# A first projection streamed into the norm before it, and masks built later, in a two-layer encoder trunk

## The reference

```
y = rms_norm(h, norm_w[0, 0])
xb, zb = split(y @ rg_w_in)                # 1024 -> 2 x 2048
xb = dwconv(xb, conv_w) + conv_b           # four taps
for d in (forward, backward):
    r, i = sigmoid(xb_blocks @ gate_w[d] + gate_b[d])       # 8 blocks of 256
    a = exp(-8 * softplus(-lam[d]) * r)
    h_d = linear_recurrence(a, sqrt(1 - a^2) * i * xb)
out = ((h_0 + h_1) * silu(zb)) @ rg_w_out
```

## Time and profile before

| | |
|---|---|
| median of 3 runs | 2765.61 us (2759.55 to 2768.03) |
| the profiled execution | 2772.26 us |
| its span in the profile | 2770.5 us |
| setup | ends at 30.0 us |
| first norm | 30.0 to 61.7 us |
| recurrent stage | 61.7 to 832.3 us |
| second norm | 832.3 to 902.1 us |
| DeltaNet projection, chunks, last norm | 902.1 us to the end |

### The profile page before, as it was taken

How to read it: one execution, slowest core, us unless ns; L and a number is a source line. 1 busy time by engine, 2 the same in 40 slices (tenths; PEclk the granted TensorE clock), 3 DMA queues, 4 the chain that set the end, 5 groups by cost and what they waited for, 6 DMA issues and landing times. The chain is left out here.

```text
span 2770.5 us, 51969 instructions
## 1 busy us (share of the span) xinstructions
PE 2569.3 (93%) x18313; PEld 2485.3 (90%) x18313; DVE 1810.4 (65%) x2713; ACT 1257.3 (45%) x2179; POOL 1215.6 (44%) x1111
## 2 busy tenths in 40 slices
PE   3999999988996999999999699999999999999994
PEld 3999999988994889999999699999999999998994
DVE  5277777777006788888888666767767777776103
ACT  4366666673013534445443345554545545465102
POOL 4333333436211255554445454545545555573320
PEclk7999999999998999999999789999999999999997
DMA  4122212123104355544454542424244241423113
GB/s 156 43 63 62 61 61 61 61 85 108 46 22 158 83 152 164 162 141 124 143 159 136 175 117 50 120 50 120 64 101 113 54 114 50 119 71 110 46 38 122
DMA packets 243118, 269.26 MB, mean 97 GB/s; under 512 B 86747, under 2 KB 210220, under 8 KB 241276
## 3 DMA queue, kind: packets, MB, share of 16 engines
q1 hardware_dynamic: 242940, 266.96, 33.5%
HBM read 182.59 MB, written 84.33 MB: 96 GB/s over the span
## 5 line engine op out<-in xcount | busy, mean ns | idle before, releaser
L649 PE MATMUL ps<-dn_yhi,dn_whi 128*128 128x348 f32 x1128 | 385.2, 341 | 8.0 <-ACT p_vrow L1548 5.3
L2281 ACT ACTIVATE zz<-ps 104x416 fp32r<-104x416 f32 x560 | 283.6, 516 | 228.6 <-PE ps L2117 226.8
L650 PE MATMUL ps<-dn_ylo,dn_whi 128*128 128x348 f32 x1128 | 363.0, 322 | 0.0
L651 PE MATMUL ps<-dn_yhi,dn_wlo 128*128 128x348 f32 x1128 | 362.9, 322 | 0.0
L2404 DVE TENSOR_TENSOR pp<-ps,level_mask 104x416 fp32r<-104x416 f32 x480 | 275.7, 588 | 132.1 <-PE ps L2117 130.1
L649 PE MATMUL ps<-rg_yhi,rg_whi 128*128 128x346 f32 (+1 forms) x960 | 310.9, 324 | 42.0 <-PEq L82 32.9
L651 PE MATMUL ps<-rg_yhi,rg_wlo 128*128 128x346 f32 (+1 forms) x960 | 310.4, 323 | 0.0
L650 PE MATMUL ps<-rg_ylo_r,rg_whi 128*128 128x346 f32 (+1 forms) x960 | 310.4, 323 | 0.0
L2119 PE MATMUL ps<-pp,zz 104*104 104x208 f32 x1440 | 267.5, 296 | 18.5 <-ACT zz L2281 9.6
L2119 PE MATMUL ps<-zz,pp 104*104 104x208 f32 x1440 | 248.4, 283 | 0.0
L649 PEld LDWEIGHTS ps<-dn_yhi,dn_whi 128*128 128x128 f32 x1128 | 213.0, 189 | 13.0 <-issue 9.6
(11 more groups left out here) (356 smaller groups left out, 7025.0 us busy)
## 6 DMA issues: line engine op xcount, KB each, us to landing
c_nq<-nq_scratch SPq DMA_DIRECT2D x160, 169.0 KB
dn_raw<-in_dn_w_in SPq DMA_DIRECT2D x48, 512.0 KB, 4.4
qd<-rows_scratch SPq DMA_DIRECT2D x160, 104.0 KB, 3.1
rg_raw<-in_rg_w_in SPq DMA_DIRECT2D x32, 512.0 KB, 4.4
nq_scratch<-p_nq SPq DMA_DIRECT2D x48, 338.0 KB
p_ex<-rows_scratch SPq DMA_DIRECT2D x32, 422.5 KB
nq_scratch<-p_rn SPq DMA_DIRECT2D x32, 338.0 KB
n_h<-h_scratch SPq DMA_DIRECT2D x16, 520.0 KB, 7.6
```

The source lines that it names most:

```text
L649: e.matmul(o, whi, mhi[:, t0:t0 + tn], start=(first and k == 0), stop=False)
L650: e.matmul(o, whi, mlo[:, t0:t0 + tn], start=False, stop=False)
L651: ins = e.matmul(o, wlo, mhi[:, t0:t0 + tn], start=False, stop=(last and k == end))
L2281: e.activation(zz[:, b, :, :], ps[0:CH, 2 * b + 1, 0:m4], ACT.Copy).then_inc(zev.sem, 1)
```

## The change

Four things change.

The weights of X0 and X1 of turn 0 are loaded in the setup, between token rows 5 and 6, and GpSimd splits them there. In the first norm PE multiplies each tile k by both units, 18 matmuls a tile, into PSUM banks 0 to 2 and 3 to 5, as soon as `rg_ylo` of that tile is written. In the same phase SyncE loads the weights of X0 and X1 of turn 1 ahead of the stores of `h_first`; they are split at the recurrent stage's start, and PE's first unit there is X0 of turn 1.

The level masks leave the setup. GpSimd builds them with the same 57 operations behind its last weight split of the recurrent stage.

The setup holds seven token rows, and ScalarE's squares alternate between two buffers.

`row_diag` is made by VectorE, behind its copy of the same row, and no longer by ScalarE.

```diff
--- before.py
+++ after.py
@@ -167,10 +167,11 @@
             with ExitStack() as s2:
                 h = sb(s2, "h_first", [P, KT, T])
                 setup(nc, sb, ps, c, x, meta_tokens, norm_w, rg_conv_w, rg_conv_b, rg_gate_b, rg_lambda,
-                      dn_conv_w, dn_norm_w, h)
+                      dn_conv_w, dn_norm_w, h,
+                      (room, [rg_w_in[0].rearrange("(k p) m -> p k m", p=P)[:, :, j * P:(j + 1) * P] for j in (0, 1)]))
                 norms(nc, sb, ps, c, "n0", h_dram, None, None, 0, 0, yhi, ylo, h=h,
                       first=(room, [rg_w_in[0].rearrange("(k p) m -> p k m", p=P)[:, :, j * P:(j + 1) * P]
-                                    for j in (0, 1)]))
+                                    for j in (2, 3)]))
             rg_loop(nc, sb, ps, c, yhi, ylo, room, rg_w_in, rg_gate_w, o_dram, rg_w_out, y, ysum, twin,
                     o_raw)
         base = (nc.sbuf_base + 31) // 32 * 32
@@ -206,13 +207,13 @@
 
 
 def setup(nc, sb, ps, c, x, meta_tokens, norm_w, rg_conv_w, rg_conv_b, rg_gate_b, rg_lambda,
-          dn_conv_w, dn_norm_w, ht):
+          dn_conv_w, dn_norm_w, ht, first):
 
     with Phase(nc) as s:
         prow = sb(s, "prow", [P, 3, P])
-        ROWS = 4
+        ROWS = 7
         hrow = sb(s, "hrow", [CH, ROWS, D])
-        junk, ssq, diag = sb(s, "row_sq", [CH, D]), sb(s, "row_ssq", [CH, NC]), sb(s, "row_diag", [CH, 2, CH])
+        junk, ssq, diag = sb(s, "row_sq", [CH, 2, D]), sb(s, "row_ssq", [CH, NC]), sb(s, "row_diag", [CH, 2, CH])
         tmp, work = sb(s, "sp_tmp", [P, 4, 32]), sb(s, "sp_work", [P, 4, 32])
         sem = lambda n: s.semaphore(n)
         par_in, masks, par_t, par_done = sem("par_in"), sem("masks"), sem("par_t"), sem("par_done")
@@ -220,6 +221,7 @@
         ident_ready, row_t, row_free = sem("ident_ready"), sem("row_t"), sem("row_free")
         row_sq, diag_done, row_sum = sem("row_sq"), sem("row_diag"), sem("row_sum")
         act_done, dve_done = sem("sp_act"), sem("sp_dve")
+        w_in, w_hi, w_lo = [sem("w_in0"), sem("w_in1")], sem("w_hi"), sem("w_lo")
         block = s.block()
 
         @block.sync
@@ -241,6 +243,10 @@
                 if k >= ROWS:
                     e.wait_ge(row_t, k - ROWS + 1)
                     e.wait_ge(row_sq, k - ROWS + 1)
+                if k == 6:
+                    for j in range(2):
+                        e.dma_start(first[0][0][:, j, :].rearrange("p (k m) -> p k m", k=KT), first[1][j]) \
+                            .then_inc(w_in[j], 16)
                 if k == 0:
                     e.dma_start(hrow[0:META, 0, :], meta_tokens).then_inc(row_in[0], 16)
                     e.dma_start(hrow[META:CH, 0, :], x[0, 0:CH - META, :]).then_inc(row_in[0], 16)
@@ -283,22 +289,12 @@
             select(gm[:, 1, 0, :], ALU.is_gt, 0.0, 0, 1, [[-1, CH]])
             select(gm[:, 0, 1, :], ALU.is_ge, 0.0, 0, -1, [[1, CH]])
             select(gm[:, 1, 1, :], ALU.is_ge, 0.0, 0, 1, [[-1, CH]])
-            lm = c["level_mask"]
-            then(e.memset(lm[:, :, :, :], 0.0))
-            for l in range(LEVELS):
-                m = 1 << l
...
-                    select(lm[:, l, d, :], ALU.not_equal, 1.0, 0, 1, [[-1, P]])
+            raw, hi, lo = first[0]
+            for j in range(2):
+                e.wait_ge(w_in[j], 16)
+                e.tensor_copy(hi[:, j, :], raw[:, j, :]).then_inc(w_hi, 1)
+                e.wait_ge(w_hi, j + 1)
+                e.tensor_tensor(lo[:, j, :], raw[:, j, :], hi[:, j, :], ALU.subtract).then_inc(w_lo, 1)
 
         @block.tensor
         def _(e):
@@ -345,6 +341,11 @@
                 src = ps[:, 2 * (k % 2):2 * (k % 2) + 2, 0:4 * CH].rearrange("p a (b t) -> p a b t", t=CH)
                 dst = ht[:, :, k * CH:(k + 1) * CH].rearrange("p (a b) t -> p a b t", b=4)
                 e.tensor_copy(dst, src).then_inc(row_free, 1)
+                e.wait_ge(row_sq, k + 1)
+                if k >= 2:
+                    e.wait_ge(row_sum, k - 1)
+                e.tensor_scalar(diag[:, k % 2, :], c["ident"][0:CH, 0:CH], ssq[:, k:k + 1], None, ALU.mult) \
+                    .then_inc(diag_done, 1)
 
         @block.scalar
         def _(e):
@@ -370,13 +371,41 @@
             e.activation(tmp[:, 2, :], lam, ACT.Relu, scale=-1.0).then_inc(act_done, 1)
             for k in range(NC):
                 e.wait_ge(row_in[k % ROWS], 16 * (k // ROWS + 1 + (k % ROWS == 0)))
-                e.activation(junk[:, :], hrow[:, k % ROWS, :], ACT.Square, accum_out=ssq[:, k:k + 1]) \
+                if k >= 2:
+                    e.wait_ge(row_sq, k - 1)
+                e.activation(junk[:, k % 2, :], hrow[:, k % ROWS, :], ACT.Square, accum_out=ssq[:, k:k + 1]) \
                     .then_inc(row_sq, 1)
-                e.wait_ge(row_sq, k + 1)
-                if k >= 2:
-                    e.wait_ge(row_sum, k - 1)
-                e.activation(diag[:, k % 2, :], c["ident"][0:CH, 0:CH], ACT.Copy, scale=ssq[:, k:k + 1]) \
-                    .then_inc(diag_done, 1)
+
+
+def level_masks(e, lm, done):
+
+
+    count = [0]
+
+    def then(ins):
+        count[0] += 1
+        ins.then_inc(done, 1)
+        e.wait_ge(done, count[0])
+
+    def select(view, op, fill, base, ch, pattern):
+        then(e.affine_select(out=view, in_=view, compare_op=op, fill=fill, base=base,
+                             pattern=pattern, channel_multiplier=ch))
+
+    then(e.memset(lm[:, :, :, :], 0.0))
+    for l in range(LEVELS):
+        m = 1 << l
+        nb = P // (2 * m)
+        v = [lm[:, l, d, :].rearrange("p (b h j) -> p b h j", h=2, j=m)[:, :, d, :] for d in (0, 1)]
+        for d in (0, 1):
+            then(e.memset(v[d], 1.0))
+
+        select(v[0], ALU.is_ge, 0.0, -m, 1, [[-2 * m, nb], [0, m]])
+        select(v[0], ALU.is_ge, 0.0, 2 * m - 1, -1, [[2 * m, nb], [0, m]])
+
+        select(v[1], ALU.is_ge, 0.0, 0, 1, [[-2 * m, nb], [0, m]])
+        select(v[1], ALU.is_ge, 0.0, m - 1, -1, [[2 * m, nb], [0, m]])
+        for d in (0, 1):
+            select(lm[:, l, d, :], ALU.not_equal, 1.0, 0, 1, [[-1, P]])
 
 
 def softplus(e, work, expo, relu, at, done):
@@ -435,7 +464,7 @@
         def _(e):
             for j in range(2) if first else ():
                 e.dma_start(first[0][0][:, j, :].rearrange("p (k m) -> p k m", k=KT), first[1][j]) \
-                    .then_inc(w_in[j], 16)
+                    .then_inc(w_next, 16)
             for k in range(KT) if yt is None else ():
                 e.dma_start(h_dram[k], ht[:, k, :]).then_inc(stored, 16)
             if ab:
@@ -447,6 +476,7 @@
                 e.dma_start(ht[:, k, :], h_dram[k]).then_inc(h_in[k], 16)
             if yt is None:
                 e.wait_ge(stored, 16 * KT)
+                e.wait_ge(w_next, 32)
             elif pre is not None:
                 for k in range(KT):
                     e.wait_ge(added, k + 1)
@@ -508,6 +538,15 @@
                                        sq[:, k % 2, t0:t0 + tn] if src is ht else ysum[:, t0:t0 + tn],
                                        start=(k == 0), stop=(k == n - 1))
                     ins.then_inc(summed, 1)
+            for k in range(KT) if first else ():
+                e.wait_ge(lo_done, k + 1)
+                for j in range(2):
+                    _, whi, wlo = first[0]
+                    for b, (t0, tn) in enumerate(EVEN):
+                        o, cols = ps[:, 3 * j + b, 0:tn], slice(k * P, (k + 1) * P)
+                        e.matmul(o, whi[:, j, cols], yhi[k][:, t0:t0 + tn], start=(k == 0), stop=False)
+                        e.matmul(o, whi[:, j, cols], ylo[k][:, t0:t0 + tn], start=False, stop=False)
+                        e.matmul(o, wlo[:, j, cols], yhi[k][:, t0:t0 + tn], start=False, stop=(k == KT - 1))
             if ab:
                 _, whi, wlo = lead[0]
                 e.wait_ge(ab_lo, 1)
@@ -570,8 +609,8 @@
                 e.wait_ge(ab_hi, 1)
                 e.tensor_tensor(ab["lo"][:, :, :], ab["raw"][:, :, :], ab["hi"][:, :, :], ALU.subtract) \
                     .then_inc(ab_lo, 1)
-            for j in range(2) if first or lead else ():
-                raw, hi, lo = (first or lead)[0]
+            for j in range(2) if lead else ():
+                raw, hi, lo = lead[0]
                 e.wait_ge(w_in[j], 16)
                 e.tensor_copy(hi[:, j, :], raw[:, j, :]).then_inc(w_hi, 1)
                 e.wait_ge(w_hi, j + 1)
@@ -676,7 +715,7 @@
 
 
     with Phase(nc) as s:
-        wt = Weights(nc, sb, s, "rg", (1, 1, 2, 2, 1, 1), 2, ahead=2, room=room, come=1)
+        wt = Weights(nc, sb, s, "rg", (1, 1, 2, 2, 1, 1), 2, ahead=2, room=room, come=2)
         (xpad, o1), (xc, o2), (zs, o15) = twin(s, "xpad", [P, 2, T + 4]), twin(s, "xc", [P, 2, T]), twin(s, "zs", [P, 2, T])
         (xhi_raw, xhi), (xlo_raw, xlo) = twin(s, "xhi", [P, 2, T]), twin(s, "xlo", [P, 2, T])
         a, u = (y[:, 4 * i:4 * i + 4, :].rearrange("p (d t) x -> p d t x", d=2) for i in (0, 1))
@@ -689,7 +728,8 @@
```

(7 more changed lines are left out.)

9 lines of the change are left out of this document (removed).

## The result

The changed kernel took 2773.0 us, the median of 20 runs (2762.1 to 2785.6), against 2765.6 for the kernel before (20 runs, 2759.6 to 2771.7). The ratio is 1.0030, with a 95% interval of 1.0022 to 1.0039: it is slower by about 0.3%, where 0.42% faster was forecast. The profiled execution took 2773.2, its span 2771.4.

What follows compares the result with a forecast made beforehand. PE was taken to bound the kernel, busy for 2569.3 of 2770.5 us. The terms -14.96 + 3.0 + 0.3 = -11.7 us took the median from 2765.61 to 2753.9, with a range of 2745 to 2764.

Steps and rivals of the forecast that it cites:

- The step that failed: Recurrent stage's start: from the first gates on, engines were taken to stand to each other as before.
- masks on the path: Recurrent stage's end: masks take 45.8 us, the stage ends 20.5 us later, 2774.4; rival's chance 0.04.
- a low clock all through the norm: First norm: PE's 144 matmuls stay at the low clock, 43.8 instead of 24.3 us, 2773.4; rival's chance 0.03.
- my sum: Whole kernel: -14.96 up to the gates, + 3.0 setup, + 0.3 masks = -11.7 us, median 2753.9.
- The setup term: Setup: two weight loads and a longer tail start the next phase 3.0 us later; bounds -0.2 and +8 us.
- a bound and a rival: Setup: VectorE's diagonals wait 2 us behind GpSimd's splits; in the +8 us bound and the 2760.2 rival, chance 0.21.
- The norm: First norm: VectorE's pair takes 2.52 us, PE starts 8.82 us in, the recurrent stage starts 35.64 us in.
- The restart: First norm: PE's start at the low clock, for nine matmuls, adds 1.30 us.
- The recurrent stage's start: There PE waits 4.05 us for GpSimd's split, then 1.30 for the clock and 22.97 of matmuls before the gates.
- This restart: Recurrent stage's start: PE's clock falls again while it waits, charged another 1.30 us.
- The masks: Recurrent stage's end: hidden by 1.4 to 2.4 us; 0.3 us charged for VectorE's two additions, bounds 0 and 3.
- the port rule: Recurrent stage's end: GpSimd and VectorE lock each other out, masks held up to 2.5 us, costing 0.1 to 1.1 more.

Runs made afterwards that it cites:

- its two forms: Changed kernel with the ten diagonals back on ScalarE, 2749.6 us; changed kernel with three one-column memsets ahead of VectorE's setup, 2757.0 us.
- the unrolled version: Changed kernel with the three turns of the chunk loop written out on every engine, so no branch goes back: 2751.7 us.

## Why the prediction was wrong

**The step that failed** is the one sentence at the end of the recurrent stage's start: "From there on all engines stand to each other as before." The sum has nothing for the chunk stage because of it. For the data flow it is nearly true. But VectorE's program was 18 instructions longer ahead of a loop that first branches back at 1874.81, and I had looked only at what instructions wait for, not at where they stand. The order of instructions of both kernels was at hand and would have given the count. None of the rivals had the mechanism; the slower ones, masks on the path (2774.4) and a low clock all through the norm (2773.4), have times that the 2773.0 comes near by chance, and neither happened. In place of the nothing, the runs showed second pauses of 5.41 and 4.53 us, and 16.0 us of time that went with them when VectorE's program was shifted by three instructions.

The two profiles give this account. 10.3 us are gained at the second norm. 3.4 are lost at three clock starts behind it, and 2.5 more at the start of the chunk stage, around which PE's clock is at its lower level for 61.4 us (from 1549.3) instead of 54.6 (from 1559.6). So the changed kernel is 4.4 ahead at the loop (1839.04 against 1843.43). 12.4 are lost at the two branches back (251.9 against 239.5). This gives 8.0 slower, and the medians say 7.4. The profiled executions themselves are only 0.9 apart, since that of the kernel before, 6.7 above its median, lost 7 us at three other steps of the chunk stage (116.7, 116.7 and 118.8 where the changed kernel has 115.1). Without the second pauses the change is worth what was forecast: 0.9943 and 0.9969 in its two forms, about 16 and 9 us, around the 11.7 of my sum. With runs of one kernel that lie 15 us apart, this bears the sum out only within some 4 us.

The Trainium skill has the rule (Runtime: NRT & Kernel Launch, on instruction fetch mechanics): the instruction memory of most engines is two blocks of 256 instructions, filled in sequence, and a taken branch to a target outside them stalls until it is fetched. The runs agree with the branch stalling (2.7 to 3.6 us on VectorE) and with a boundary that matters to one instruction; the length of a block no run here measured. Nor does a loop's length alone say whether it pays: ScalarE's of 460 instructions, fewer than two such blocks would hold, paused for 2.4 to 2.7 us, and GpSimd's of 287 did not. The Trainium skill calls the cost of crossing a boundary in that same section mostly hidden, and the unrolled version agrees, with no issue wait at `head_pair`. The second stall of a loop's head close to a boundary, which decides this case, rests on the runs alone. The prediction drew on none of this.

**The setup term**, forecast 3.0, measured 3.23, by a partly different way. Row 9 was there by 27.39 instead of 28.3, but the tail behind it took 5.1 us (27.39 to 32.52) instead of 3.4. Row 6 landed 4.7 us behind row 5, where the rows before it came 1.9 apart: SyncE's issue of the second weight load took 4.20 us and that of row 6 5.76. Rows 6 to 9 then came 1.1 to 1.5 us apart, and PE needed 1.8 for each: eight transposes took it 1.59 in rows 6 to 8, where those of row 8 took 0.93 in the kernel before. In the changed kernel with the diagonals on ScalarE they took 1.54, 1.65, 0.88 and 0.93, and the norm began at 31.98. One diagonal of VectorE also took 1.85 us instead of 0.27, beside GpSimd's split; the prediction had this only in a bound and a rival. The same loads and splits gave norm starts of 31.98 to 34.45 in other kernels, so the setup is loose by 2.5 us.

**The norm.** VectorE's pair took the 2.52 forecast, and PE began at 41.96 (forecast 41.8). The restart was sized too small: the first 18 matmuls, not 9, ran at the lower level, 5.37 us from 41.96 to 47.33, which costs 5.37 - 18 x 0.1595 = 2.50 instead of 1.30. PE ended at 67.57 (66.3), and the stage began at 69.86 (68.6).

**The recurrent stage's start.** The wait for GpSimd's split is there and as forecast: PE's first matmul 3.77 us into the stage (4.05). The first gate came at 98.67 (97.0). This restart was sized too small as well: from PE's first matmul to the gate it was 98.67 - 73.63 = 25.04, which is 2.07 above the 22.97 at the higher level, where 1.30 was charged. The gain at this point was 10.3, forecast 11.7 + 0.3.

**The masks** are hidden. GpSimd ended at 819.18 and the last addition still took 1.24 us, so the 0.3 I charged was zero, and the further price of 0.1 to 1.1 by the port rule did not appear. What the prediction cites as that rule agrees with the trace: the addition before the last (817.36) ran beside the last six selects, took its 1.24 us all the same, and the six took 3.03 instead of the 2.03 of the setup. So the masks were held for 1.0 us, where up to 2.5 was allowed, and still ended before the last addition began.

**What I had no term for** is the phase of the clock. The second norm's and the next projection's starts found it in another state than before, for the same work. Before, then after (874 to 879 answers to 865 to 870, and 902 to 903 to 894 to 896):

```profile
874.00:879.00 5.00, 4.86 (x21) 3.46 (x22) 5.00 (x5) 2.15 (x2) 0.00 (x0) 0.71 0.02 3
...
902.00:903.00 1.00, 0.46 (x3) 0.46 (x4) 0.75 (x5) 0.69 (x3) 0.60 (x3) 1.00 0.00 0
```

```profile
865.00:870.00 5.00, 5.00 (x18) 3.98 (x17) 5.00 (x5) 2.15 (x2) 0.00 (x0) 0.50 0.01 3
...
894.00:896.00 2.00, 1.73 (x6) 1.73 (x7) 1.90 (x8) 1.96 (x5) 1.67 (x3) 0.50 0.07 11
```

The offset between the two kernels shrank there from 10.33 to 6.93 us, in steps of 0.7, 1.3 and 1.3.

## What to carry to other kernels

Count the instructions that an edit puts ahead of each long loop, engine by engine, also where the edit is in another stage: VectorE's loop of 646 instructions paid for its branch back, and twice when its head stood 1 or 3 instructions ahead of a block's end. When a change loses time at a loop whose code it does not touch, and the wait's releaser is "issue", shift the program by a few empty instructions before looking for a cause in the work. If the turns are few, write them out.
